# The last experts in turns half as long, and the layer's gate on rows that go straight into x

## The reference, cut to what matters

```python
def moe_swiglu(h, w_router, w_gate, w_up, w_down):
    ...
    top_vals, top_idx = lax.top_k(logits, TOP_K)
    top_w = jax.nn.softmax(top_vals, axis=-1)
    gates = jnp.sum(jax.nn.one_hot(top_idx, N_EXPERTS_2, dtype=jnp.float32) * top_w[..., None], axis=1)
    out = jnp.zeros_like(t)
    for e in range(N_EXPERTS_2):
        out = out + gates[:, e:e + 1].astype(t.dtype) * swiglu(t, w_gate[e], w_up[e], w_down[e])
    return out.reshape(bsz, seq, d)
...
        x = x + g2[:, None, :] * y
    return rmsnorm(x, final_norm)
```

## Time and profile before

| | us |
|---|---|
| median of 3 runs | 2312.49 (2307.22 to 2314.65) |
| the profiled execution's own time | 2311.4 |
| its span | 2309.5 |
| PE busy in the span | 1952.6 (85%) |
| DVE busy | 1085.1 (47%) |
| ACT busy | 854.1 (37%) |
| read from HBM | 659.90 MB, 286 GB/s over the span |

### The profile page before, as it was taken

The page is one execution under the profiler, slowest core; times in us unless marked ns, Lnnn a source line. Parts: engine busy times, 40 slices in busy tenths (PEclk is TensorE's granted clock), DMA queues, the critical chain, the costliest instruction groups (busy, mean ns, idle before and its releaser), DMA issues.

```text
span 2309.5 us, 29186 instructions
## 1 busy us (share of the span) xinstructions
PE 1952.6 (85%) x12033; PEld 1401.9 (61%) x12033; DVE 1085.1 (47%) x1661; ACT 854.1 (37%) x1153; POOL 44.9 (2%) x110
## 2 busy tenths in 40 slices
PE   6989988996656556698999998998987999997996
PEld 6968767762111111357899797877843775843772
DVE  3945556431211110233555577767830873930772
ACT  4432344310000000234444357846710754720760
POOL 0010200000000000000000000000000000000000
PEclk9989998999898888899999999999999999999998
DMA  8463662489999999859445454407999999999996
GB/s 269 168 219 110 210 244 74 189 315 393 409 409 409 409 409 409 302 198 369 147 165 201 164 155 160 143 1 286 367 383 405 406 372 409 391 379 405 407 379 244
DMA packets 227523, 663.02 MB, mean 287 GB/s; under 512 B 20100, under 2 KB 28840, under 8 KB 227124
## 3 DMA queue, kind: packets, MB, share of 16 engines
q1 hardware_dynamic: 219628, 652.92, 74.0%
q10 hardware_dynamic: 7752, 8.11, 1.3%
HBM read 659.90 MB, written 1.10 MB: 286 GB/s over the span
## 4 chain that ended last, share of the span: by engine, by line
PE 52%; DMA 25%; DVE 12%; ACT 7%; issue 3%; POOL 0%; ACTq 0%; SPq 0%; DVEq 0%; POOLq 0%
PE psum L263 11%; PE psum L265 11%; PE psum L264 11%; PE psum L252 6%; DMA ring<-in_w_expert_down 6%; DMA ring<-in_w_expert_up 5%; DMA ring<-in_w_expert_gate 5%; DMA ring<-in_moe_w_gate 4%; PE psum L2458 3%; DMA ring<-in_moe_w_up 3%; PE psum L2513 2%; DVE w_lo L202 2%; PE psum L2738 2%; ACT w_hi L192 2%; PE psum L1175 1%
## 5 line engine op out<-in xcount | busy, mean ns | idle before, releaser
L202 DVE TENSOR_TENSOR w_lo<-ring,w_hi 128x1024 fp32r<-128x1024 f32 (+1 forms) x498 | 579.4, 1187 | 389.4 <-ACT w_hi L192 380.6
L192 ACT CAST w_hi<-ring 128x1024 fp32r<-128x1024 f32 (+1 forms) x498 | 502.9, 1021 | 335.8 <-PE psum L265 297.0
L2738 PE MATMUL psum<-ring,hT 128*32 128x512 f32 x960 | 145.5, 738 | 117.1 <-DMA ring<-in_w_expert_gate 63.8
L2458 PE MATMUL psum<-ring,xg_pair 128*64 128x512 f32 (+1 forms) x768 | 159.8, 561 | 38.8 <-DMA ring<-in_moe_w_gate 19.9
L2738 PEld LDWEIGHTS psum<-ring,hT 128*32 128x32 f32 x960 | 30.3, 124 | 228.0 <-issue 97.5
L263 PE MATMUL psum<-w_hi,xg_hi 128*128 128x512 f32 (+1 forms) x384 | 146.4, 381 | 7.3 <-DVE w_lo L202 7.3
L264 PE MATMUL psum<-w_hi,xg_lo 128*128 128x512 f32 (+1 forms) x384 | 145.1, 378 | 0.0
L265 PE MATMUL psum<-w_lo,xg_hi 128*128 128x512 f32 (+1 forms) x384 | 144.8, 377 | 0.0
L2458 PEld LDWEIGHTS psum<-ring,xg_pair 128*64 128x64 f32 x768 | 58.9, 137 | 136.7 <-issue 134.8
L2372 DVE TENSOR_TENSOR x<-x,psum 128x1024 f32<-128x1024 f32 x14 | 17.1, 1221 | 219.8 <-PE psum L252 219.8
L2760 PE MATMUL psum<-ring,midT 128*32 128x512 f32 x480 | 69.9, 712 | 44.0 <-DMA ring<-in_w_expert_down 43.5
(11 more groups left out here) (697 smaller groups left out, 3799.0 us busy)
## 6 DMA issues: line engine op xcount, KB each, us to landing
ring<-in_moe_w_down SPq DMA_DIRECT2D x88, 1024.0 KB, 7.9
ring<-in_w_expert_gate SPq DMA_DIRECT2D x32, 2048.0 KB, 17.2
ring<-in_moe_w_gate SPq DMA_DIRECT2D x64, 1024.0 KB, 13.2
ring<-in_moe_w_up SPq DMA_DIRECT2D x64, 1024.0 KB, 14.5
ring<-in_w_expert_down SPq DMA_DIRECT2D x30, 2048.0 KB, 18.1
...
```

The costliest lines, as they stand in the source:

```text
L192: a.copy(self.buffers(n, src.shape)[0], src).then_inc(*self.hi_made.up())
L202: v.tensor_tensor(lo, src, hi.bitcast(F32), SUB).then_inc(*self.lo_made.up())
L2458: ins = p.matmul(ps[r, cut], moe2.xg_pair[:, i - HEAVY, k0 + k, r], w[side][:, k, cut], start=k0 + k == 0, stop=k0 + k == KD - 1)
L2738: ins = p.matmul(ps[slots_of(j), g * 512:(g + 1) * 512], M.xg[:, 2 * q + k, slots_of(j)], w[:, j, k, :], start=2 * q + k == 0, stop=2 * q ...
```

## The change

Two things change.

**The order.** `PHASES` becomes `STEPS`, whose entries are single chunks (0, 1, 2) or the down projection (`OUT`). A large expert comes in two halves: chunks 0 and 1, then chunk 2 and the down projection. After each half stands one chunk or the down projection of a pair. All functions of the stage take one step where they took one phase; the units are loaded in the order of the steps. The splits of a large expert's weights reach ahead only to the end of its half, and after each chunk of a pair the first four parts of the next half are split. The two products that gather the pairs' tokens (`light_step_pe`) stand one chunk earlier.

**The layer's gate.** The rows of an expert are multiplied by the token's gate and the layer's gate in one VectorE instruction (`y_gated`, in what was `total`), which reads the products from PSUM. ScalarE and VectorE then split `y_gated` from SBUF. The spread rows are added to x. The two instructions of 128 by 2048 behind the last expert go, and GpSimd's zeroing of `total` too. Twelve products of a constant (`constant_products`), whose results nobody reads, stand before the last scatter on TensorE.

```diff
-PHASES = (("in", 0), ("out", 0), ("in", 4), ("in", 1), ("out", 1), ("out", 4),
-          ("in", 2), ("out", 2), ("in", 5), ("in", 3), ("out", 3), ("out", 5))
+OUT = 3
+STEPS = ((0, 0), (0, 1), (4, 0), (0, 2), (0, OUT), (4, 1), (1, 0), (1, 1), (4, 2), (1, 2), (1, OUT), (4, OUT),
+         (2, 0), (2, 1), (5, 0), (2, 2), (2, OUT), (5, 1), (3, 0), (3, 1), (5, 2), (3, 2), (3, OUT), (5, OUT))
...
-    moe2.gain8, moe2.acc = None, total
+    moe2.gain8, moe2.acc = None, x
+    y_gated = total[:, 0, :]
...
     def y_hi_act(a, run, i):
         M, st = run.moe, run.st
-        a.wait_ge(*st.dve.of("selgT", i))
-        a.activation(M.y_split[0], run.banks.of(st.name, "down", i), ACT.Copy, scale=M.slot_gate[:, 0:1]).then_inc(*st.act.up("y", i))
+        a.wait_ge(*st.dve.of("y_gated", i))
+        a.copy(M.y_split[0], y_gated).then_inc(*st.act.up("y", i))
...
+    def y_gated_dve(v, run, i, multiplied):
+
+        M, st = run.moe, run.st
+        v.wait_ge(*multiplied)
+        v.wait_ge(*gates_loaded.of("layer", 1))
+        v.wait_ge(*st.dve.of("selgT", i))
+        v.scalar_tensor_tensor(y_gated, run.banks.of(st.name, "down", i), M.slot_gate[:, 0:1], gate_b[:, 1, :], MUL, MUL).then_inc(*st.dve.up("y_gated", i))
+        run.banks.empty(st.dve, st.name, "down", i)
...
-        v.scalar_tensor_tensor(M.y_split[1], run.banks.of(st.name, "down", i), M.slot_gate[:, 0:1], M.y_split[0].bitcast(F32),
-                               MUL, SUB).then_inc(*st.dve.up("y_lo", i))
-        run.banks.empty(st.dve, st.name, "down", i)
+        v.tensor_tensor(M.y_split[1], y_gated, M.y_split[0].bitcast(F32), SUB).then_inc(*st.dve.up("y_lo", i))
...
-                if i == 0 and ch == 1:
-                    light_step_pe(p, g)
...
+            if (i, ch, g) == (0, 0, 1):
+                light_step_pe(p, 0)
+            if (i, ch, g) == (0, 1, 0):
+                light_step_pe(p, 1)
...
+        constant_products(p, banks.held_by("moe2", "selgT", OUTS[-1])[:, 512:1024], ident, 12)
         banks.let_go("moe2", "down", OUTS[-1])
         scatter_pe(p, run2, OUTS[-1])
...
-    def hi_after(a, i, u):
-        fine_split.make_hi(a, min(fine_split.end(u) + PARTS, fine_split.end(out_unit(i))))
+    def hi_after(a, i, ch, u):
+        fine_split.make_hi(a, min(fine_split.end(u) + PARTS, step_end(*heavy_end(i, ch))))
...
+        if i < HEAVY:
+            lo_after(v, i, ch, in_unit(i, 1, ch))
+        else:
+            fine_split.make_lo(v, parts_ahead(i, ch, 1))
...
+        banks.empty(d, "moe2", "up", i, ch)
+        if (i, ch) == (HEAVY, 0):
+            ranked_table_dve(v, st, M)
         if i >= HEAVY:
-            fine_split.make_lo(v, parts_ahead("in", i, PARTS))
+            fine_split.make_lo(v, parts_ahead(i, ch, PARTS))
...
-        g.wait_ge(*S["moe2"].dve.of("hT", 4))
-        g.memset(total[:, :, :], 0.0).then_inc(*S["moe2"].pool.up("total"))
...
-        settle(v, v.tensor_tensor(total[:, :, :], total[:, :, :], gate_b[:, 1, :].unsqueeze(1).to_broadcast([P, NT, D]), MUL), d)
-        settle(v, v.tensor_tensor(x[:, :, :], x[:, :, :], total[:, :, :], ADD), d, "x")
...
-        a.wait_ge(*st.dve.of("x"))
+        a.wait_ge(*S["moe2"].dve.of("acc", OUTS[-1], 0))
```

More of the change, by code:

```diff
@@ L2605, in ranked_act @@
             pair_step_act(a, 0, step)
-        for phase, i in PHASES:
-            (in_act if phase == "in" else out_act)(a, i)
+        for i, ch in STEPS:
+            if ch == OUT:
+                out_act(a, i)
+            else:
+                in_act(a, i, ch)
         over_act(a, run2, over2)
```

218 lines of the change are left out of this document (113 added, 105 removed).

## The result

| | before | after |
| --- | --- | --- |
| median of the runs, us | 2312.25 (2307.22 to 2314.65, 4 runs) | 2295.80 (2293.88 to 2297.53, 4 runs) |
| profiled execution, us | 2311.4 | 2297.53 |
| its span | 2309.5 | 2295.7 |
| first product of an expert (PE L263) | 1587.06 | 1586.44 |
| from there to the end of the span | 722.4 | 709.3 |

The ratio is 0.993, 95% interval 0.9917 to 0.9944: 13 to 19 us faster. The forecast was 2292 in a range of 2283 to 2303.

What follows compares the result with a forecast made beforehand. The prediction took the weight loads, paused whenever the ring is full, as the bound. Loads -15.1 us and the end -4.9 sum to -20.0; from 2311.4 plus 1.1 that gives 2292 us, range 2283 to 2303.

Steps and rivals of the forecast that it cites:

- quiet as forecast: Where a pair's step follows a half expert: lead stays under 16.8 us, so the seam costs nothing, four places excepted.
- (a): Loads at every seam: the ring has room to spare, all 24.9 us come back, 2282 us; chance together with 2288 0.15.
- (c): Seams: each costs the same however little lead there is, so eight cost 30 us, kernel slower at 2322; chance 0.05.
- (d): Loads do not end sooner, HBM gives the rate back elsewhere; only the end's -4.9 us, 2308; chance 0.06.
- (b): Lead not drained after a pair's chunk, or six quiet seams lose 1.5 us each: half the gain, 2301; chance 0.18.
- the one long stretch at 400 GB/s: Sign of being right: loads at 400 GB/s or more from 1700 us to the last load.
- The end: Behind the last expert product: y 1.2 us more, scatter 1.4 less, the 128 by 2048 instructions 4.7 less: -4.9 us.
- The loads: Weight loads over the stage: 9.8 us lost to a full ring against 24.9 before, a gain of 15.1 us.
- now stands between the pair's chunk and the splits, and PE waits for it: 5.0 + 4.9 + 6.0 + 3.5: Expert 0's half B: the 4.9 us table on VectorE makes PE wait, lead reaches 19.4 us, 2.6 us lost.
- eight units (20.6 us) are worth 16.8: Ring of weight loads: it bears a lead of only 16.8 us, 3.8 of its 20.6 us being of no use.
- Five more experts pay this too, behind the next step's gate products, where the scatter has some 10 us of cover.: y's extra 1.2 us at five more experts: some 10 us of cover for the scatter behind the next step's gate products.
- the prediction's paragraph on the ring: The skill's fixed 2.0 us per load would make the ring bear 18.6 us, estimate 4.6 us faster; the sum kept 16.8.

Runs made afterwards that it cites:

- e6: The changed kernel with a ring of seven units instead of eight: 2307.70 us, 0.9986 of the kernel before.
- e9: The changed kernel with a ring of nine units, the ninth in the unused buffer of the sums: 2287.37 us, 0.9882 of the kernel before.
- e1: The kernel before, its order kept, with only the layer's gate on the rows and the twelve constant products: 2308.35 us, 0.9988 of the kernel before.
- e2: The changed kernel with the ranked table's 27 instructions moved ahead of the pair's low part and the wait for silu: 2288.19 us, 0.9904 of the kernel before.
- e4: The changed kernel without the twelve constant products before the last scatter: 2296.86 us, 0.9944 of the kernel before.
- e3: The changed kernel with both pairs' chunks 1 and 2 exchanged, so the short chunk of 768 stands behind half B: 2295.85 us, 0.9939 of the kernel before.
- e8: The changed kernel with the table formed early and pair 4's first chunk already behind expert 0's first chunk: 2292.39 us, 0.9918 of the kernel before.
- e12: The changed kernel with nine units, the table early, and y formed only after the next four weight tiles are split: 2286.01 us, 0.9884 of the kernel before.
- e5: The changed kernel run again without any edit, on another chip: 2298.98 us, 0.9949 of the kernel before.

## Why the prediction was right, and where its sizes were off

**The mechanism holds.** Loads stop when the ring is full, the stage ends with the last load, and shorter turns keep the ring from filling: e6, e9 and e1 show it from three sides, with stage times that follow the loss to within some 2 us. Three of the eight seams are quiet as forecast. Rival (a), all 24.9 us back, fails on 17.0 still lost; (c) fails on the three quiet seams; (d) fails on e1 against the changed kernel. (b) put the gain of the loads near what came (half of 15.1; 8.8 were measured). Its sign, a wait for `w_lo` of more than 3 us at a restart, came at one restart of seven (5.73 us), for the table that stood there and not for the restart itself, which e2 shows; before the first product of a half PE waited 0.1 to 1.3 us, not 2.1. The three quiet seams lose nothing.

**Part of the hit is luck.** The parts come to -13.4 us where -20.0 were forecast. The median fell by 16.4, which is 3 us more than the stage, and nothing in the traces accounts for these 3 (the two profiled executions differ by 13.9). Of the signs of being right, those of the end came true; the one long stretch at 400 GB/s did not, and the last load came some 9 us sooner, not 15.

**The end, -4.9 forecast, -4.6 measured.** y in 3.72 us (3.78 forecast), the granted clock 1.0 in the scatter, the 128 by 2048 instructions gone. The products are worth 0.9 us and not 1.4, since without them the clock falls only part of the way through the scatter (e4).

**The loads, -15.1 forecast, -8.8 measured.** Three terms of the sum were mis-sized:

- "now stands between the pair's chunk and the splits, and PE waits for it: 5.0 + 4.9 + 6.0 + 3.5", 2.6 us lost. PE's wait was 5.73 us and not 4.9 less what the lead covers, and the products behind it ran at 1.2 GHz for some 5 us, which the step left out. Half B took 59.0 us, 9.2 more than the 49.8 in the sum (its siblings took 51.0 to 51.6). Lost there: 5.6 us in the changed kernel, and e2 shows 5.4 of stage and 7.2 of loading for the table in all.
- "eight units (20.6 us) are worth 16.8", at every seam. Before a chunk of 768 the units are smaller, and eight of them hold 15.5 us. The seams behind half A of experts 1 and 3 were forecast at 0 and lost 2.2 and 3.5 us; e3 moved those losses.
- "Five more experts pay this too, behind the next step's gate products, where the scatter has some 10 us of cover." The scatter has its cover, but on VectorE the weights' next low parts are queued behind y. At pair 4 that made PE's wait 2.94 us and not 1.42, and the granted clock fell again; with the scatter, half A of expert 2 took 52.3 us instead of 50.0, filled the ring, and lost 2.9 us where 0.5 was forecast. Where the clock did not fall behind the same wait (e3, e8), it took 50.9 and lost 1.5 and 1.4 (345 GB/s from 1985 to 1995, 369 from 1975 to 1990).

**The ring's account, set right.** Counted from the packets of the weights' queue alone (bytes loaded so far less the bytes of the turns that PE has ended, over 407 GB/s; the rates in the window rows take in another 0.55 MB of the stage that are not weights), the turns are, all but the last row of the changed kernel:

| turn | lead at its start | PE, us | loading, us | lead + growth + 3.5 less 20.6 | lost |
| --- | --- | --- | --- | --- | --- |
| expert 0, A | 10.0 | 49.9 | 41.2 | 1.6 | 3.5 |
| expert 0, B | 5.8 | 59.0 | 43.8 | 3.9 | 5.6 |
| 1, B | 4.9 | 51.0 | 43.8 | -5.0 | 0 |
| 2, A | 6.9 | 52.3 | 41.2 | 0.9 | 2.9 |
| 2, B | 4.9 | 51.6 | 43.8 | -4.4 | 0 |
| expert 3 whole, before | 7.2 | 97.3 | 85.0 | 2.4 | 4.0 |

A ring that fills loses the excess over its 20.6 us and 1.6 to 2.0 us besides, so it is worth 18.6 to 19.0 us and not 16.8. The prediction got 16.8 because it put the lead of expert 3 at 5.0 us, counted in units that had landed. By packets it was 7.2: a unit's landing comes some 1.8 us behind its last packet (the median of the 280 loads of this stage in the kernel before), and the next unit is on its way by then. The lead was 2.2 us too low and the dead time some 2 too high, from the same seam, so that the two cancel for a half A, which begins 7 us ahead; a half B begins 5 us ahead and has 2 us more room than forecast.

For small units the same sum with the ring's 15.5 us gives 6.9 + 6.2 + 2.6 - 15.5 = 0.2 and 7.2 + 6.3 + 2.6 - 15.5 = 0.6 (2.6 is three quarters of 3.5), with 2.2 and 3.5 lost, 2.0 and 2.9 more. With seven units e6 bore 13.0 + 3.5 = 16.5 and 12.5 + 3.5 = 16.0 us of its 18.0 and lost 0.6 and 0.1, so there too the last 2 us are of no use.

The Trainium skill's fixed cost of about 2.0 us for each load (page DMA: Bandwidth & Descriptors, section "Anatomy of one DMA — SWDGE (gpsimd) path", measured on GpSimd's path, while these loads come from SyncE) gives an estimate of 18.6 us for eight large units, and losses of 3.6, 5.9, 0, 2.9, 0 and 4.4 us in the rows of the table; for seven units it leaves 16.0 us, and 0.5 and 0 lost at e6's two seams. The trace agrees, to 0.4 us; at the two seams with small units the figure gives 2.2 and 2.6 where 2.2 and 3.5 were lost. So the prediction's paragraph on the ring had the better figure in hand and put it aside for 16.8; the difference between its two sums is also 4.1 us (1.8 + 1.8 + 0.5), not 4.6.

A part of the 2 us can be seen at a seam, here behind half A of expert 2, where the pair's first product starts at 1986.94:

```profile
1990.64 0.89 SPq L139 DMA_DIRECT2D ring<-in_moe_w_up  x2
...
1990.40:1991.60 1.20, 1.20 (x8) 0.43 (x6) 0.00 (x0) 0.00 (x0) 0.00 (x0) 1.00 0.00 0
```

SyncE issues the next load 3.7 us behind the seam, as the prediction had it (3.5), but the first packet moves at 1991.66, 1.0 us behind the issue. At the four seams of the kernel before it is the same: 3.7 to 3.8 us to the issue, 4.7 to 4.9 to the first packet.

**Open.** The rest of the 2 us, and the 2.9 at expert 3's half A, are not traced to a place. Whether to move y behind the splits is worth anything would need more executions of e12 than one profile. The changed kernel's gain was 16.4 us in the first runs and 12 in e5's, and in the profiled stages it is 13.
